# The first pass of a streamed transformer layer: the decode sample's tail moved ahead of the first tile's, and the gather ring opened by seven places

## The reference

```python
x = x + out                                   # residual after the mixers
h = rms(x, ln2_g)
q = (h @ wq).reshape(blk, 8, 128)             # queries of 8 heads, wq is 1024 x 1024
s1 = einsum('thd,hnd->thn', q[..., :64], subkeys[:, 0])   # key scores, 128 keys each half
s2 = einsum('thd,hnd->thn', q[..., 64:], subkeys[:, 1])
# top 16 of each half, top 16 of the 256 sums, expert e = i1 * 128 + i2, g = softmax
a = gelu(einsum('td,thkd->thk', h, u[e]))     # u[e]: 16 gathered rows per head
x = x + einsum('thk,thkd->td', g * a, v[e])
```

## Time and profile before

| what | value |
|---|---|
| median of 3 runs (range) | 1853.51 us (1849.15 to 1854.36) |
| the profiled execution's own time | 1854.23 us |
| its span, first to last instruction | 1852.4 us |
| PE busy | 1268.1 us (68%) |
| DVE busy | 1315.2 us (71%) |
| ACT busy | 565.0 us (30%) |
| POOL busy | 526.7 us (28%) |
| transfers | 697.51 MB, of these 570.53 MB gathers |

### The profile page before, as it was taken

The page is one execution under the profiler, slowest core; times in us unless marked ns, Lnnn a source line. Parts: engine busy times, 40 slices in busy tenths (PEclk is TensorE's granted clock), DMA queues, the critical chain, the costliest instruction groups (busy, mean ns, idle before and its releaser), DMA issues.

```text
span 1852.4 us, 26337 instructions
## 1 busy us (share of the span) xinstructions
PE 1268.1 (68%) x8990; PEld 700.3 (38%) x8990; DVE 1315.2 (71%) x3906; ACT 565.0 (30%) x1997; POOL 526.7 (28%) x569
## 2 busy tenths in 40 slices
PE   8889848667877666768877486878877444534343
PEld 4667613334544322445545133555545111111111
DVE  5562296889866586898766567998767768786754
ACT  2331123423322233334423233333423222222222
POOL 0100032333332222322322322422323333333332
PEclk9988859678888768777898687887999555555555
DMA  6224499999999999999999999998999999999997
GB/s 259 88 92 135 150 378 400 403 425 425 417 424 423 423 423 391 412 425 378 402 424 422 422 407 416 409 404 317 412 422 424 425 426 426 426 426 421 426 424 307
DMA packets 119668, 697.51 MB, mean 377 GB/s; under 512 B 18015, under 2 KB 21150, under 8 KB 49390
## 3 DMA queue, kind: packets, MB, share of 16 engines
q0 software_dynamic: 78848, 570.53, 74.0%
q1 hardware_dynamic: 36974, 122.88, 17.3%
q10 hardware_dynamic: 3712, 2.43, 0.4%
HBM read 692.70 MB, written 3.02 MB: 376 GB/s over the span
## 4 chain that ended last, share of the span: by engine, by line
DMA 33%; PE 29%; DVE 23%; issue 6%; ACT 4%; POOL 1%; DVEq 0%; POOLq 0%; ACTq 0%
DMA rows<-in_peer_uv,index 24%; DVE rows L2339 10%; PE ps_v L1600 6%; PE ps_f L1422 4%; DMA wch<-in_w_row 3%; PE ps_f L1451 3%; PE ps_f L1472 3%; PE ps_f L1216 3%; DMA wch<-in_w_out 2%; PE ps_h L1580 2%; DMA wch<-in_peer_wq 2%; PE ps_f L1340 2%; PE ps_f L1300 1%; PE ps_f L1437 1%; ACT diag L1902 1%
## 5 line engine op out<-in xcount | busy, mean ns | idle before, releaser
L1193 POOL DMA_INDIRECT rows<-in_peer_uv,index x544 | 516.8, 950 | 1226.6 <-PE ps_v L1600 1011.9
L2339 DVE CUSTOM_DVE_ANT_0 rows<-rows,ps_h 128x1024 f32<-128x1024 f32 x544 | 658.2, 1220 | 279.0 <-DMA rows<-in_peer_uv,index 214.1
L1600 PE MATMUL ps_v<-rows,diag 128*32 128x256 f32 x4352 | 433.0, 511 | 447.6 <-ACT diag L1902 436.5
L1600 PEld LDWEIGHTS ps_v<-rows,diag 128*32 128x32 f32 x4352 | 126.8, 132 | 699.5 <-ACT diag L1902 569.2
L1893 ACT ACTIVATE tan<-arg 128x2 f32<-128x2 f32 x272 | 55.4, 204 | 891.1 <-DVE arg L2349 846.7
L1896 ACT ACTIVATE weight<-tan,lead 128x1 f32<-128x1 f32 x544 | 180.8, 379 | 9.1
L1902 ACT ACTIVATE diag<-sel,weight 128x32 f32<-128x32 f32 x544 | 140.7, 305 | 0.0
L1422 PEld LDWEIGHTS ps_f<-bufh,wch 128*128 128x128 f32 x768 | 113.7, 232 | 22.7 <-issue 20.8
L1422 PE MATMUL ps_f<-bufh,wch 128*128 128x128 f32 x768 | 120.3, 321 | 0.0
L1216 PE MATMUL ps_f<-wch,bufh 128*128 128x512 f32 (+1 forms) x192 | 83.2, 576 | 16.2 <-DMA wch<-in_w_row 16.1
L1451 PE MATMUL ps_f<-wch,bufb 128*128 128x512 f32 x96 | 52.6, 687 | 17.4 <-DMA wch<-in_w_out 17.4
(11 more groups left out here) (359 smaller groups left out, 1697.9 us busy)
## 6 DMA issues: line engine op xcount, KB each, us to landing
wch<-in_w_gate SPq DMA_DIRECT2D x60, 512.0 KB
wch<-in_w_row SPq DMA_DIRECT2D x36, 512.0 KB
wch<-in_w_o SPq DMA_DIRECT2D x32, 512.0 KB
wch<-in_w_out SPq DMA_DIRECT2D x32, 512.0 KB
wch<-in_peer_wq SPq DMA_DIRECT2D x32, 512.0 KB
rows<-in_peer_uv,index POOLq DMA_INDIRECT x544
w_tok<-in_w_tok SPq DMA_DIRECT2D x4, 1640.0 KB, 13.1
wch<-in_w_uq SPq DMA_DIRECT2D x6, 384.0 KB
```

The costliest lines, as they stand in the source:

```text
L1193: pool.indirect_dma_start(rows[c % RING][:, :, :].rearrange("p a d -> p (a d)"), None, io.peer_uv[:, :], at).then_inc(s_uv[c % RING], 16)
L1600: ins = nc.tensor.matmul(ps_v[GROUP * a:GROUP * (a + 1), :], diag[:, c % DRING, :], rows[c % RING][:, 1, QD * a:QD * (a + 1)], start=False ...
L2339: v.tensor_tensor_reduce(out=u, in0=u, in1=ps_h[:, :], scale=1.0, scalar=0.0, op0=ALU.mult, op1=ALU.add, accum_out=dots[:, c % KEEP:c % KE ...
```

## The change

It does five things, all in pass 0 but for the order of the ring.

- `out` signals the sample's last matmuls by a semaphore of their own (s_y0). DVE makes the sample's residual and sum, then the tile's residual, then the sample's norm, then the tile's sum and norm.
- PE transposes the sample's rows first. A new `first_ask(b)` makes the sample's queries of four heads (half b) from four wq chunks in the slots, 32 columns a matmul, into ps_v; it doesn't release the slots. `first_ask(0)` and the sample's scores of half 0 (now in ps_h) stand ahead of the tile's transposes; `first_ask(1)` stands between `ask` 3 and `ask` 4, and half 1's scores behind `ask` 4. `ask` works on the tile's 128 columns alone.
- `first_asked(b)` copies a half's queries out in one instruction; `first_scores_out(h)` is one copy.
- `spread(0)` waits for s_sc and the stream's `residual(0)` for s_q0, since ps_h and ps_v hold the sample's scores and queries first.
- The ring's list of places is turned so that the two places over `qh0`, `sc0`, `wide_h` and `key0` come last; LATE becomes 7, so columns 0 to 6 wait for nothing but their indices.

```diff
-LATE = 4
+EARLY = 4
+LATE = RING - 2
+    m.rows = m.rows[0:EARLY] + m.rows[EARLY + 2:] + m.rows[EARLY:EARLY + 2]
...
+                            if k == DC - 1:
+                                ins.then_inc(s_y0, 1)
...
+            def first_ask(b):
+                pe.wait_ge(s_h2, 2)
+                if b:
+                    pe.wait_ge(s_q0, b)
+                for a in range(GROUPS):
+                    w = use(0, Q_AT + GROUPS * b + a)[:, :].rearrange("p (c k) -> p c k", c=DC)
+                    for k in range(DC):
+                        ins = nc.tensor.matmul(ps_v[:, GROUP * a:GROUP * (a + 1)], w[:, k, :], wide_h[:, k, at_of(0)],
+                                               start=(k == 0), stop=(k == DC - 1))
+                ins.then_inc(s_v0, 1)
...
             def ask(p, n):
-                    ins = nc.tensor.matmul(ps_f[:, 2 + n % 2, 0:x], w[:, k, :], h_of(p)[:, k, 0:x],
+                    ins = nc.tensor.matmul(ps_f[:, 2 + n % 2, 0:P], w[:, k, :], h_of(p)[:, k, 0:P],
...
             def key_scores(p, i, g, heads=range(PH2)):
-                pe.wait_ge(s_qc, PH * p + GROUPS * (heads[-1] + 1))
+                if i:
+                    pe.wait_ge(s_qc, PH * (p + 1))
+                else:
+                    pe.wait_ge(s_q0, heads[-1] + 1)
...
+                            if i == 0:
+                                into = ps_h[GROUP * a:GROUP * (a + 1), 512 * k + at:512 * k + at + NKEY]
...
                     if k == at.rows:
-                        for i in members:
-                            turn_rows(i)
+                        if p == 0:
+                            turn_rows(0)
+                            first_ask(0)
+                            key_scores(0, 0, 0, range(1))
+                        turn_rows(members[-1])
                     if at.ask <= k < at.ask + PH:
                         ask(p, k - at.ask)
+                        if p == 0 and k == at.ask + GROUPS - 1:
+                            first_ask(1)
                         if p == 0 and k == at.ask + GROUPS:
-                            key_scores(p, 0, 0, range(1))
+                            key_scores(0, 0, 0, range(1, PH2))
...
+            def first_asked(b):
+                act.wait_ge(s_v0, b + 1)
+                nc.scalar.copy(qh0[:, b:PH:PH2, :], ps_v[:, 0:P].rearrange("p (a k) -> p a k", a=GROUPS)).then_inc(s_q0, 1)
...
-                for k in range(2):
-                    ins = nc.scalar.copy(sc0[:, 0, h, k, :], ps_f[:, key_bank(0, 0, k), NKEY * h:NKEY * (h + 1)])
-                ins.then_inc(s_sc, 1)
+                both = ps_h[:, :].rearrange("p (a k) -> p a k", a=2)
+                nc.scalar.copy(sc0[:, 0, h, :, :], both[:, :, NKEY * h:NKEY * (h + 1)]).then_inc(s_sc, 1)
...
-                        for i in members:
-                            residual(p, i)
+                        if p == 0:
+                            residual(p, 0)
+                            square(0)
+                        residual(p, members[-1])
+                        if p == 0:
+                            norm(p, 0)
+                        square(members[-1])
                     if k == at.res + 1:
-                        for i in members:
-                            norm(p, i)
+                        norm(p, members[-1])
```

More of the change, by code:

```diff
@@ L800, in places @@
     m.rows = [pl(f"rows{i}", [P, 2, D]) for i in range(RING)]
+    m.rows = m.rows[0:EARLY] + m.rows[EARLY + 2:] + m.rows[EARLY:EARLY + 2]
     assert pl.at <= m.end, (pl.at, m.end)
     m.ring = pl.at - RING * 2 * D * 4
-    m.late = pl.at - (RING - LATE) * 2 * D * 4
+    m.late = pl.at - (RING - EARLY) * 2 * D * 4
     first = Plan(nc, m.ring)
@@ L819, in places @@
     m.key0 = first("key0", [P, D])
-    assert first.at <= m.cached, (first.at, m.cached)
+    assert first.at <= m.cached and first.at <= m.late + 2 * 2 * D * 4, (first.at, m.cached)
 def stream(nc, io, m, sem):
@@ L1075, in stream @@
         s_mt = sem("s_mt")
-        s_y = sem("s_y")
+        s_y0 = sem("s_y0")
+        s_v0 = sem("s_v0")
+        s_q0 = sem("s_q0")
         s_res = sem("s_res")
@@ L1786, in columns @@
                     nc.scalar.copy(h_of(p)[:, 4 * j:4 * j + 4, at_of(i)], src).then_inc(s_h2, 1)
+            def first_asked(b):
+                act.wait_ge(s_v0, b + 1)
+                nc.scalar.copy(qh0[:, b:PH:PH2, :], ps_v[:, 0:P].rearrange("p (a k) -> p a k", a=GROUPS)).then_inc(s_q0, 1)
             def asked(p, n):
                 act.wait_ge(s_wu[slot_of(p, Q_AT + n)], uses_of(p, Q_AT + n))
-                for i in PASSES[p]:
-                    ins = nc.scalar.copy(asked_of(i)[:, ASKED[n], 0:queries(i)], ps_f[:, 2 + n % 2, at_of(i)])
-                ins.then_inc(s_qc, 1)
+                nc.scalar.copy(qh[:, ASKED[n], :], ps_f[:, 2 + n % 2, 0:P]).then_inc(s_qc, 1)
             def scores_out(i, g):
@@ L1799, in scores_out @@
                     act.wait_ge(s_used, n)
-                nc.scalar.copy(sc_of(i)[:, g, :, :, :], key_banks(i, g)).then_inc(s_sc, 1)
+                nc.scalar.copy(sc_of(i)[:, g, :, :, :], key_banks(g)).then_inc(s_sc, 1)
             def first_scores_out(h):
@@ L1866, in front @@
                     if k == at.rows + 1:
-                        for i in members:
-                            columns(p, i)
+                        if p == 0:
+                            columns(p, 0)
+                            first_asked(0)
+                            first_scores_out(0)
+                        columns(p, members[-1])
                     if at.ask + 1 <= k < at.ask + 1 + PH:
                         asked(p, k - at.ask - 1)
+                        if p == 0 and k == at.ask + GROUPS:
+                            first_asked(1)
                         if p == 0 and k == at.ask + GROUPS + 1:
-                            first_scores_out(0)
-                    if p == 0 and k == at.key + 1:
-                        first_scores_out(1)
+                            first_scores_out(1)
                     if k == at.key + 1 or k == at.key + 2:
```

40 lines of the change are left out of this document (22 added, 18 removed).

## The result

The changed kernel is slower: 1867.78 us median of 7 runs (1865.14 to 1878.11), the kernel before 1849.15 in its 7 (1843.96 to 1854.36). The ratio is 1.0107, 95% interval 1.0086 to 1.0128. I had forecast 1849.0 and given "slower" a chance of 0.09. The profiled execution took 1878.11 us, the longest of its seven, with a span of 1876.3; so times are compared by medians, and the trace is read for stretches.

What follows compares the result with a forecast made beforehand. It took the gather stream's start, and whether it runs dry, to bound the kernel. A 5.1 us lead off the profiled 1854.2 gave 1849.1, from the median 1848.4; forecast 1849.0, own range 1846 to 1852, wider range 1842.5 to 1857.

Steps and rivals of the forecast that it cites:

- part 1: Tail of pass 0: indices come earlier, DVE's choice starting 13.0 us sooner (bounds 10.4 to 16.3), first_ask(0) taking 6.8 us.
- the dots: DVE's dot products at the end of pass 0, first one forecast at 249.6, bounds 1.5 us earlier or later.
- The head start: DVE's choice of indices in pass 0 starts at 213.7, 13.0 us earlier than 226.70; first gather at 224.0.
- The third rival: Gathers meet wq loads in pass 0; one late load delays the dot products 8.2 us, so slower; chance 0.12.
- A hole opened in the transfers: Sign that the forecast is right: transfer engines idle between 253 and 257, until the tenth gather's data.
- a lead: Bytes transferred ahead in the gather stream after the change: 2.17 MB, at 426 GB/s 5.1 us.
- the rule C: Theory made after the trace: time is 1848.6 + (last output matmul's end to first dot product - 49.8) - 5.
- The dot products hardly move: Part 3, end of pass 0: first_choose(1) still waits for ACT's softmax, so no change, first dot product at 249.6.

Runs made afterwards that it cites:

- the one with four gathers ahead: Changed kernel with both first_ask turned round and the softmax behind the fourth query copy, but column 4 instead of 7 waits for s_used: 1848.03 us.
- a_warm: Changed kernel with eight extra unused matmuls of 512 columns, so that PE has no idle stretch ahead of first_ask(0): 1868.74 us.
- a_late_gathers: Changed kernel, but POOL's first gather also waits until both halves of the sample's queries are made: 1870.4 us.

## Why the prediction was wrong

**The step that failed is the price of `first_ask` in part 1.** I reckoned 64 instructions at 0.107 us, 6.8 us at the clock of 1.2 GHz. The count and the clock were right; the series took 13.86 us, 13.86 / 64 = 0.217 us each. At 2.4 GHz I took 0.054; the run with the warm clock shows 53 instructions in 5.70 us, 0.11 each. So my bound of 3.5 to 6.8 us didn't hold the truth at either clock. I had read the price from transposes with 32 and 48 rows of data, and a matmul here has 128. The tile's transposes, with 128 rows, stand in the next line of the earlier trace rows: eight in 1.97 us, with the same tail of 0.3 some 0.21 each. Whether the rows or the kind of instruction halves the price no run separates.

At full clock a narrow query (16 instructions, some 1.8 us) is as dear as one of 128 columns (ACT's copies of the tile's follow each other by 1.79 us): `first_ask` adds 16 instructions per head, and the 32 columns that it takes out of `ask` save a fifth of a wide one.

The Trainium skill's page TensorE: Matmul & The Clock Gate, section LDWEIGHTS, puts a weight load at its columns divided by 1.2, in ns; an estimate from that is 6.8 us for the 64 loads. At 2.4 GHz the 0.11 us measured makes 7.0 and agrees. The 13.86 us at 1.2 GHz are twice that estimate; here the measurement decides.

**What it did to the dots, against the reckoning.** I had them at 249.6; they came at 273.15, 23.5 us later:

| piece | reckoned | measured | later by |
|---|---|---|---|
| `first_ask(0)` begins | 205.6 | 206.34 | 0.7 |
| `first_ask(0)` | 6.8 | 13.86 | 7.1 |
| to the tile's first query | 2.7 | 3.6 | 0.9 |
| queries 0 to 3 | 7.0 | 9.2 | 2.2 |
| `first_ask(1)` with its wait | 3.9 | 12.9 | 9.0 |
| queries 4 to 7 and scores of a half | 7.4 | 10.7 | 3.3 |
| from there to the dots | 16.2 | 16.5 | 0.3 |

**The clock was a second error.** I let it rise by 211 to 214, as after the wide queries of before. It stayed at half until the tile's queries had run for 4 us, at 228, and fell again inside `first_ask(1)`. That is in the queries 0 to 3, in the last head of `first_ask(1)` (3.62 us) and in query 4, 3.76 us where 1.74 were reckoned. It is not in `first_ask(0)`, which I had priced at the low clock. The head start shrank from 13.0 us to 4.8.

**The third rival happened in part, and is the smaller part.** `ask(3)` ended at 233.0 instead of 222.1, the gathers went at 232.2, and chunk 7 landed 9.3 us after its release, where 3.0 were reckoned alone and 11.15 beside gathers. So the collision was there and its size near the row's. But PE waited 3.92 us for it, the kernel without that wait had its dots only 2.5 us sooner and was no faster, and the rival's 8.2 us for the dots are not what made up 23.4. Its condition, a slip of `ask(3)` against the first gather, I tied to a low clock alone and gave 0.12.

By the rule of the Trainium skill's page DMA: Bandwidth & Descriptors, section Queues, rings and completion order, I had 2.5 us for this load. That was the time of the bytes alone, and it took the packets of both queues as equally large, an assumption of mine. With what a load alone takes beyond its bytes (3.0 less 0.52 MB at 425 GB/s, 1.2), half the rate makes an estimate of 4.3 us; the measured 9.3 doesn't agree.

**What held.** The sample's norm ended at 204.3 (204.0 reckoned). Seven gathers followed at 1.25 us. Columns 7 and 8 waited for `first_choose(1)`. A hole opened in the transfers. The dots' start sets the time less a lead: over the versions the rule C holds within 6 us, but for the one with four gathers ahead (changed: 1867.0 reckoned, 1867.8 measured). By that rule the lead is 3.7 us on the average of ten versions, where 5.1 were reckoned, and from -1 to 8 us in the single ones; as each has one profiled run and a median, its size is not shown better than that.

**What the price alone doesn't explain.** "The dot products hardly move" fell with the price, but not with it alone. With the turned matmuls and nothing else `first_ask(0)` cost 3.64 us, less than I had reckoned, and the dots still came 5.2 us later than before. From the end of `ask(3)` to query 4 that run needed 9.0 us where 3.9 were reckoned, 4.70 of them the wait for chunk 7, which this form needs at once. Only with the softmax moved as well did the dots come earlier than before, by 0.8 to 5.6 us.

**What stays open.** Why PE stands still under "issue" in some runs while gathers move (about 1.5 us in each of four versions, 3.3 us in the one shown); whether seven free places beat four by 3 us; and which part of the turned form's gain is due to the few weight columns and which to the four column groups, as no version has one without the other. That narrow matmuls are what lets the clock fall rests on where it fell, in two versions and the changed kernel; nothing was run that changes only that.

## What to carry to other kernels

Price a matmul from a row with the same kind of instruction, the same rows and the same weight columns, at both clocks, before moving a few of its columns elsewhere: 32 moving columns under 128 weight columns cost as much as 128 here. If few columns are on one side, make them the weights and lay four such matmuls into four column groups. When work is brought forward, look first at what its consumer waits for in program order behind it: here one softmax behind all copies was worth 10 us by itself. And where a load is asked for only when its slot comes free, look at what its reader can do meanwhile, and price it beside the stream that may have started by then.

## What the runs showed of the hardware

- Back-to-back matmuls of 32 columns under 128 weight columns kept PE busy for 13.9 us and its clock stayed at 1.2 GHz. The clock fell from 2.4 GHz inside such a series, with PE busy, in the changed kernel (at 238.2), in a_warm (213.0 and 233.5) and in a_late_gathers (232.6). In the changed kernel it had risen at 228, 4 us into the tile's queries with 128 moving columns.
- An instruction of 32 moving columns under 128 weight columns took 0.217 us at 1.2 GHz and 0.11 at 2.4.
- The turned form, 64 instructions with 32 weight columns in four column groups, took 3.64 us at 1.2 GHz wherever PE was not held up, 0.057 each.
- A 512 KB load took some 3.0 us from the release of its slot alone, 4.5 us where gathers began 1.8 us after its release, and 9.3 us where the first gather had been issued 1.0 us before it.
